# Queries, keys and probabilities of the forgetting heads turned in 32x32 blocks and carried through DRAM

## The reference, cut to what matters

```python
fq = rms_norm(fq.reshape(B, S, FOX_HEADS, 128), fox_q_g)   # queries, normed
fk = rms_norm(fk.reshape(B, S, FOX_HEADS, 128), fox_k_g)   # keys, normed
c = jnp.cumsum(log_sigmoid(flog + b_forget), axis=1)
s_f = einsum('bhqd,bhkd->bhqk', fq_b, fk_h) * fox_scale + cq_b[..., :, None] - ck[..., None, :]
p_f = softmax(where(causal, s_f, NEG_INF), axis=-1)
o_f = einsum('bhqk,bhkd->bhqd', p_f, fv_h)
```

## Time and profile before

| | us |
|---|---|
| median of 3 runs (1050.15 to 1050.65) | 1050.58 |
| the profiled execution | 1050.27 |
| its span, first to last instruction | 1048.5 |
| TensorE busy | 1044.0 |
| ScalarE busy | 778.0 |
| VectorE busy | 756.2 |

### The profile page before, as it was taken

The page is one execution under the profiler, slowest core; times in us unless marked ns, Lnnn a source line. Parts: engine busy times, 40 slices in busy tenths (PEclk is TensorE's granted clock), DMA queues, the critical chain, the costliest instruction groups (busy, mean ns, idle before and its releaser), DMA issues.

```text
span 1048.5 us, 16983 instructions
## 1 busy us (share of the span) xinstructions
PE 1044.0 (100%) x5495; PEld 950.2 (91%) x5495; DVE 756.2 (72%) x1259; ACT 778.0 (74%) x1334; POOL 35.8 (3%) x43
## 2 busy tenths in 40 slices
PE   9999999999999999999999999999999999999998
PEld 9999999999999988888888888888889988888887
DVE  7788877777668764586776776777767678777664
ACT  7777676888856544879788788797787778758853
POOL 0101020000002210000000000000000000000000
DMA  9755565565656666566665665665655766656664
GB/s 358 232 163 172 182 206 186 161 198 164 225 197 193 207 201 202 193 212 200 195 219 190 198 218 189 213 204 192 219 180 190 236 202 202 204 195 214 205 204 143
DMA packets 66939, 211.35 MB, mean 202 GB/s; under 512 B 9272, under 2 KB 10432, under 8 KB 66752
## 3 DMA queue, kind: packets, MB, share of 16 engines
q1 hardware_dynamic: 66880, 210.57, 62.0%
HBM read 208.43 MB, written 2.11 MB: 201 GB/s over the span
## 4 chain that ended last, share of the span: by engine, by line
PE 97%; ACT 1%; DVE 1%; issue 0%; DMA 0%; SPq 0%; DVEq 0%; ACTq 0%
PE ps L547 14%; PE ps L548 14%; PE ps L549 14%; PE ps L343 7%; PE ps L345 7%; PE ps L344 7%; PE ps L585 7%; PE ps L583 7%; PE ps L584 7%; PE ps L350 5%; PE ps L351 3%; PE ps L369 1%; PE ps L378 1%; ACT w_hi L631 1%; PE ps L454 0%; ACT qkT L677 0%
## 5 line engine op out<-in xcount | busy, mean ns | idle before, releaser
L1058 DVE TENSOR_TENSOR w_lo<-raw,w_hi 128x1024 fp32r<-128x1024 f32 (+1 forms) x406 | 463.4, 1148 | 228.0 <-ACT w_hi L631 225.5
L631 ACT ACTIVATE w_hi<-raw 128x1024 fp32r<-128x1024 f32 (+1 forms) x406 | 400.1, 988 | 182.5 <-PE ps L549 65.0
L547 PE MATMUL ps<-w_hi,xs 128*128 128x512 f32 (+1 forms) x704 | 263.5, 374 | 0.0
L548 PE MATMUL ps<-w_lo,xs 128*128 128x512 f32 (+1 forms) x704 | 263.4, 374 | 0.0
L549 PE MATMUL ps<-w_hi,xs 128*128 128x512 f32 (+1 forms) x704 | 263.4, 374 | 0.0
L343 PE MATMUL ps<-w_hi,xs 128*128 128x384 f32 (+1 forms) x512 | 172.6, 337 | 0.0
L344 PE MATMUL ps<-w_lo,xs 128*128 128x384 f32 (+1 forms) x512 | 167.0, 326 | 0.0
L345 PE MATMUL ps<-w_hi,xs 128*128 128x384 f32 (+1 forms) x512 | 167.0, 326 | 0.0
L549 PEld LDWEIGHTS ps<-w_hi,xs 128*128 128x128 f32 x704 | 133.1, 189 | 17.2
L548 PEld LDWEIGHTS ps<-w_lo,xs 128*128 128x128 f32 x704 | 133.1, 189 | 17.2
L547 PEld LDWEIGHTS ps<-w_hi,xs 128*128 128x128 f32 x704 | 133.1, 189 | 17.1
(11 more groups left out here) (158 smaller groups left out, 948.9 us busy)
## 6 DMA issues: line engine op xcount, KB each, us to landing
raw<-in_wrest SPq DMA_DIRECT2D x278, 512.0 KB, 4.1
raw<-in_win SPq DMA_DIRECT2D x117, 384.0 KB, 3.5
raw<-in_wrest SPq DMA_DIRECT2D x16, 384.0 KB, 3.0
xtok<-in_xtok SPq DMA_DIRECT2D x4, 512.0 KB, 13.5
raw_ahead<-in_w SPq DMA_DIRECT2D x5, 392.0 KB, 7.9
xv<-in_xT SPq DMA_DIRECT2D x7, 256.0 KB, 7.5
out<-x_tok SPq DMA_DIRECT2D x7, 256.0 KB, 4.3
raw_ahead<-in_win SPq DMA_DIRECT2D x3, 384.0 KB, 8.4
```

Of the source, the lines that this page charges most:

```text
L547: pe.matmul(o, xh, wh, start=(k == 0), stop=False, skip_group_check=True)
L548: pe.matmul(o, xh, wl, start=False, stop=False, skip_group_check=True)
L631: act.activation(slot(w_hi, s, w), slot(raw, s, w), ACT.Copy).then_inc(hi_ready, 1)
L1058: dve.tensor_tensor(slot(w_lo, s, w), slot(raw, s, w), f32(slot(w_hi, s, w)), ALU.subtract).then_inc(split_done, 1)
```

## The change

- Head 9 joins the scheme of blocks: it is turned by VectorE, no longer by TensorE, and its steps get the places of the other block heads. Scores move from after piece 5 to after piece 6.
- `norm_apply` writes the queries and keys with the four 32-column groups outermost, so that each group's blocks are contiguous after the turn. `turn_qk` moves behind the split of b = 7.
- The 16 copies of `move_qk` go. ScalarE instead issues one DMA of the turned tile to DRAM (`store_qk`, after the split of b = 1), waits for it, and issues four DMAs back, one per group of 32 partitions (`load_qkT`, b = 2). The keys are read by the scores as they land; the queries are copied once into a contiguous tile (`copy_q`, b = 4).
- The probabilities of heads 9 to 14 are no longer turned by TensorE: `normalise` writes them in block order, VectorE turns them (`turn_p`, at b = 7 between `norm_stats` and `norm_apply`), SP stores them to DRAM and loads them back in four DMAs (`store_p`, `load_pT`), in between its loads of weights, and the values are multiplied after piece 4 of the next frame instead of piece 1. Head 15's probabilities stay with TensorE.
- SP's loop over the weight pieces is written out from piece 76 on.

```diff
-BLOCK_AT = dict(scores=5)
-MOVES = {1: (0, 5), 2: (5, 10), 3: (10, 15)}
-FOX1_AT = dict(turn=2, scores=3, probs=6, values=7)
+BLOCK_AT = dict(scores=6)
+QK0, P_STOP = H + 1, HEADS - 1
...
+            def store_p(f):
+                sp.wait_ge(p_turned, blocks_counted(f))
+                if f > QK0:
+                    sp.wait_ge(pT_landed, 64 * blocks_counted(f - 1))
+                sp.dma_start(p_d, pdT[:]).then_inc(p_stored, 16)
+
+            def load_pT(f):
+                sp.wait_ge(p_stored, 16 * blocks_counted(f))
+                sp.wait_ge(pv_done, f - 1)
+                for j in range(4):
+                    src = p_d[:, j * 3 * 32:(j + 1) * 3 * 32].rearrange("(i r) c -> r i c", i=4)
+                    sp.dma_start(pT[32 * j:32 * (j + 1), :].rearrange("r (i c) -> r i c", i=4), src).then_inc(pT_landed, 16)
+
+            one_piece(8 * QK0 + 4)
+            one_piece(8 * QK0 + 5)
+            for f in range(QK0, HEADS):
+                one_piece(8 * f + 6)
+                if f > QK0:
+                    store_p(f - 1)
+                    load_pT(f - 1)
+                for g in range(8 * f + 7, 8 * f + 14):
+                    one_piece(g)
...
+            def block_scores(f):
+
+                pe.wait_ge(qkT_ready, f)
+                k = qkT[:].rearrange("p (i n m t) -> p n m i t", i=4, m=M, n=2)[:, 1]
+                for qb in range(M):
+                    last = pe.matmul(bank(B_S, qb * P, (qb + 1) * P), qT[:, qb * P:(qb + 1) * P], k[:, 0:qb + 1], start=True,
+                                     stop=True, skip_group_check=True)
+                last.then_inc(s_done, 1)
+
+            def block_values(f, p):
+
+                pe.wait_ge(pT_landed, f * 64 - 64 * (QK0 - 1))
+                pe.wait_ge(mixlo_done, f - 1)
...
-                    if spill and b == 0:
-                        prob_transposes(f - 1, "fox")
-                    if spill and b == 1:
-                        values(f - 1, par, "fox")
+                    if spill and b == 4:
+                        block_values(f - 1, par)
...
+            def store_qk(f):
+                act.wait_ge(qk_turned, f - (QK0 - 1))
+                if not (isinstance(f, int) and f == QK0):
+                    act.wait_ge(qk_landed, f * 64 - 64 * QK0)
+                act.dma_start(qk_d, qnT[:]).then_inc(qk_stored, 16)
+
+            def load_qkT(f):
+                act.wait_ge(qk_stored, f * 16 - 16 * (QK0 - 1))
+                act.wait_ge(s_done, f - 1)
+                for j in range(4):
+                    src = qk_d[:, j * 4 * 32:(j + 1) * 4 * 32].rearrange("(i r) c -> r i c", i=4)
+                    act.dma_start(qkT[32 * j:32 * (j + 1), :].rearrange("r (i c) -> r i c", i=4), src).then_inc(qk_landed, 16)
+
+            def copy_q(f):
+
+                act.wait_ge(qk_landed, f * 64 - 64 * (QK0 - 1))
+                turned = qkT[:].rearrange("p (i n m t) -> p n m i t", i=4, m=M, n=2)
+                act.activation(qT[:].rearrange("p (m i t) -> p m i t", m=M, i=4), turned[:, 0], ACT.Copy).then_inc(qkT_ready, 1)
...
                     if b == 7:
                         evacuate(f * 8 + 8, par, par)
-                        if next_kind == "diff" or blocks:
-                            head_norm(f + 1, next_kind)
...
+                        head_norm(f + 1, next_kind)
                     split_next(f, b, PW if last and b >= 4 else W1)
...
+                    if at is BLOCK_AT and b == 1:
+                        store_qk(f)
+                    if at is BLOCK_AT and b == 2:
+                        load_qkT(f)
+                    if at is BLOCK_AT and b == 4:
+                        copy_q(f)
+                    attention_steps(f, kind, b, at)
                     if trail:
                         trailing_steps(f, b)
...
+            def turn_p(f):
+
+                dve.wait_ge(p_ready, f)
+                if not (isinstance(f, int) and f == QK0):
+                    dve.wait_ge(p_stored, f * 16 - 16 * QK0)
+                dve.transpose(pdT[:], pd[:]).then_inc(p_turned, 1)
...
                 for b in range(8):
-                    before_split(f, kind, b, at, trail)
+                    before_split(f, kind, b, at, trail, p_blocks)
                     if b == 7:
                         norm_stats(f + 1, next_kind)
-                        norm_apply(f + 1, 1 - p, next_kind)
-                        if turn:
-                            turn_qk(f + 1, 1 - p)
+                        if p_blocks:
+                            turn_p(f)
+                        norm_apply(f + 1, 1 - p, next_kind, blocks=turn)
...
                     split_next(f, b, PW if last and b >= 4 else W1)
+                    if turn and b == 7:
+                        turn_qk(f + 1, 1 - p)
```

More of the change, by code:

```diff
@@ L301, in _, with one_piece @@
                          ).then_inc(cq_landed, 16)
-            with sp.Fori(17, IN_PIECES // RING) as i:
+            with sp.Fori(17, 2 * QK0 + 1) as i:
                 in_pieces(i)
+            def one_piece(g):
+                sp.wait_ge(split_done, g - RING + 1)
+                if g < IN_PIECES:
+                    sp.dma_start(slot(raw, g % RING, W1), win_d[(g - 8) * P:(g - 7) * P, :]).then_inc(raw_landed[g % RING], 16)
+                else:
+                    sp.dma_start(slot(raw, g % RING), wrest_d[(g - IN_PIECES) * P:(g - IN_PIECES + 1) * P, :]
+                                 ).then_inc(raw_landed[g % RING], 16)
+            def store_p(f):
[18 more added lines that the diff above has]
+                    one_piece(g)
+            one_piece(OUT0 + 6)
+            one_piece(OUT0 + 7)
             sp.dma_start(conv[:], vec_d).then_inc(conv_landed, 16)
@@ L371, in scores @@
                 last.then_inc(s_done, 1)
+            def block_scores(f):
[8 more added lines that the diff above has]
+                pe.wait_ge(mixlo_done, f - 1)
+                v = [qkv[:, (p * M + m) * QKV + 2 * HD:(p * M + m + 1) * QKV] for m in range(M)]
+                turned = pT[:].rearrange("p (i s t) -> p s i t", i=4, s=3)
+                pe.matmul(bank(B_O, 0, S), v[0], turned[:, 0:2], start=True, stop=False, skip_group_check=True)
+                pe.matmul(bank(B_O, P, P), v[1], turned[:, 2], start=False, stop=True,
+                          skip_group_check=True).then_inc(pv_done, 1)
             def prob_transposes(f, kind):
@@ L417, in attention_steps @@
                 if b == at["scores"]:
-                    scores(f, kind)
+                    if at is BLOCK_AT:
+                        block_scores(f)
+                    else:
+                        scores(f, kind)
                 if b == at.get("probs"):
@@ L498, in _ @@
                 frame(f, f % 2, "diff", DIFF_AT, trail=True, late=f == 4, forget=f == 5)
-            frame(H + 1, 1, "fox", FOX1_AT, trail=True)
-            frame(H + 2, 0, "fox", BLOCK_AT)
+            frame(H + 1, 1, "fox", BLOCK_AT, trail=True)
+            frame(H + 2, 0, "fox", BLOCK_AT, spill=True)
             with pe.Fori(H // 2 + 1, H - 1) as i:
@@ L662, in copy_qkT @@
             def copy_qkT(f, kind):
-                act.wait_ge(tp_done, H + 2 if isinstance(f, int) and f == HEADS else f)
+                act.wait_ge(tp_done, H + 1 if isinstance(f, int) and f == HEADS else f)
                 if kind == "fox":
@@ L759, in split_next, with frame @@
                 split_hi(f * 8 + (b + 4), b % RING, f * 2 + (2 + b // 4), w)
-            def frame(f, par, kind, next_kind, at=None, trail=False, last=False, forget=False, blocks=False, spill=False):
+            def frame(f, par, kind, next_kind, at=None, trail=False, last=False, forget=False, spill=False):
                 for b in range(8):
@@ L1121, in norm_apply @@
                         src = qkv[:, (p * M + m) * QKV + j * w:(p * M + m) * QKV + (j + 1) * w]
+                        gain = row[:, R_FG + j * w:R_FG + (j + 1) * w]
                         i = m * 2 + j
-                        last = dve.scalar_tensor_tensor(
-                            out=qn[:, (p * 2 * M + i) * w:(p * 2 * M + i + 1) * w], in0=src, scalar=rs[:, i:i + 1],
-                            in1=row[:, R_FG + j * w:R_FG + (j + 1) * w], op0=ALU.mult, op1=ALU.mult)
+                        to = qn[:, (p * 2 * M + i) * w:(p * 2 * M + i + 1) * w]
+                        if blocks:
+                            src, gain = [a.rearrange("p (j t) -> p j t", j=4) for a in (src, gain)]
+                            to = qn[:, p * 2 * M * w:(p + 1) * 2 * M * w].rearrange("p (j n t) -> p n j t", j=4, n=2 * M)[:, j * M + m]
+                        last = dve.scalar_tensor_tensor(out=to, in0=src, scalar=rs[:, i:i + 1], in1=gain, op0=ALU.mult,
+                                                        op1=ALU.mult)
                 last.then_inc(normed, 1)
@@ L1158, in normalise @@
                         lo, w = qb * P, P * (1 + qb)
-                        last = dve.tensor_scalar(s_sb[:, lo:lo + w], s_sb[:, lo:lo + w], rl[:, qb:qb + 1], None, ALU.mult)
```

(5 more changed lines are left out.)

73 lines of the change are left out of this document (31 added, 42 removed).

## The result

The changed kernel takes 1074.4 us (median of 6 runs) against 1050.62, a ratio of 1.0226 with a 95% interval of 1.0212 to 1.0240. The forecast was 1049.3. One of the six took 1368.4 us at a mean granted clock of 0.753, where the others had 0.990 to 0.995; it is left out of the ratio, and the other five alone have a median of 1073.8. The span of the profiled execution is 1073.1 us, 24.6 more than before.

The account below looks back on a forecast made before the run. TensorE, busy 1044.0 of 1048.5 us, was taken as the bound. 1050.27 - 2.42 (transposes) - 0.3 (late copies) + 1.45 (wait at head 8's end) = 1049.0, plus 0.3 for the runs' median: 1049.3 us, range 1047.6 to 1054.

Parts of the forecast that it names:

- What TensorE sheds: TensorE's stream: 22 transposes go, 2.42 us, and a wait of 0.3; scores and values in block order cost nothing extra.
- rival D: TensorE: each transpose is worth its whole record, 0.27 us, 22 of them 6.0, giving 1045.7 us; chance 0.02.
- What VectorE gets: VectorE at a frame's end: turn of probabilities 0.53 us added; the split of b = 7 keeps a lead of 0.65.
- Rival C: VectorE's lead at b = 7 is gone; TensorE waits 0.1 to 0.65 us per frame, 1049.9 to 1053.2; chance 0.17.
- The probabilities' way: SP's store and four loads back: store 2.2 us, landing 2.5, in time for the values with a lead of 1.3.
- Head 8's end: Frame 9: ScalarE's guess comes behind store and loads, so TensorE waits 1.45 us before transposing head 8's result.
- The queries' way: ScalarE's store and four loads back of queries and keys: copied near E+12.5, needed at E+14.3, lead 1.8 us.
- E: Time origin of the forecast's deadlines: the end of a frame's last piece on TensorE, just before ScalarE's squares start.
- head 10's late copies: TensorE's wait for ScalarE's 16 late copies at the first head, 0.3 us, claimed to go with the copies.
- covered by 3 us: SP's next weight load, delayed by the probabilities' transfers, lands at E+9.5 to 10 and is still in time by 3 us.
- Rival B: Slow read-back from DRAM: probabilities land late, TensorE waits 2.15 us at the values in six frames, 1062 us; chance 0.12.

Follow-up runs that it names:

- e2: Changed kernel with only the probabilities of heads 9 to 14 through DRAM; queries and keys by TensorE and ScalarE's 16 copies as before: 1050.5 us, ratio 1.0001.
- e6: e2 with head 15 in its old places (queries and keys turned before the split, scores after piece 5): 1050.35 us, ratio 1.0000.
- e3: Changed kernel with weight pieces 76 to 127 loaded only in their first 96 of 768 columns: 1052.6 us, single execution.
- e12b: Changed kernel with weight pieces 76 to 127 loaded only in 384 of 768 columns: 1053.25 us, single execution.
- e1: Changed kernel with only queries and keys through DRAM; probabilities of 9 to 15 turned by TensorE as before: 1062.7 us, ratio 1.0112.
- e5: Changed kernel with the queries' store and read-back moved to SP's queue, among its weight loads: 1065.4 us, ratio 1.0136.
- e7: Changed kernel with 6 matmuls into an unused bank in front of each TensorE wait for the queries: 1072.3 us, ratio 1.0199.

## Why the prediction was wrong

**What TensorE sheds: right.** 0.33 us per frame, measured in e2. A transpose is worth 0.11 us of path, not its record (rival D falls). Scores and values cost the same in block order (0.67 and 0.66 us; e2).

**What VectorE gets: right.** The lead at b = 3 was narrow and held, though the turn of the probabilities took 0.58 us, not 0.53: 0.2 us was lost once in e2, and 0.73 where both turns stood ahead of the split (e6). Rival C is real but was not in the changed kernel's list of waits.

**The probabilities' way: right, and better.** Store 1.9 us (2.2 forecast), read-back 1.9 (2.5).

**Head 8's end: right in place and cause, short in size.** 2.1 us in place of 1.45. Four issues took 1.78 us (1.65), but they began at 177.34, not 175.95: the store of the first head took 3.4 us to land, not 2.2, again beside three weight loads (2.1 in e3, with thin ones). That would have made nearly 3 us of wait. That it was only 2.1 is in part luck: head 8's values, six matmuls that take 0.66 us of TensorE at the start of frame 9, are missing from the forecast's "after five pieces at 168.1 + 9.75", and TensorE came that much later too.

**The queries' way: the step that failed.** ScalarE "issues four loads until E+9.7, which have landed near E+12", with a lead of 1.8. All but the landing came true: in the frame shown above (E = 208.5) the loads left from E+8.2 to E+10.1, but the last landed at E+17.1. The term of 2.5 us for a landing was an estimate from transfers that ran alone. It measured 5.6 us by the median and up to 7.4, and the waits were 14.2 us in six heads; the 0.3 us credited for head 10's late copies turned into one of them. Two things were left out. The loads share the engines with the weights, and e3, e12b and the changed kernel show the landing rising from 2.2 over 3.5 to 5.6 us as the weights do. And the probabilities' detour, which the forecast checked only for its own deadline and the weights' ("covered by 3 us"), holds the weights back until they leave together, just ahead of these loads; e1 puts that at 1.2 us of landing and about half of the waits. The forecast counted DMA time in the weights' direction only, never what weights do to a small transfer. The DMA engines' share of 0.65 in these frames, not much over 0.59, gave no warning: a mean over a frame says nothing of the three microseconds in which one transfer has to pass.

The Trainium skill's "DMA: Bandwidth & Descriptors" (Issuing engines are not separate DMA queues) says that DMAs started by different engines run on the same 16 DMA engines and interleave. The trace agrees (5.6 us beside the weights, 2.2 without), and weighed in the forecast it would have asked for just this term.

**Rival B: the right kind, the wrong transfer.** It gave 1062 for a slow way back, with 0.12, and put it on the probabilities. Its threshold of 3.8 us is that of the probabilities (2.5 and their lead of 1.3), and they stayed below it; the same sum for the queries gives 2.5 + 1.8 = 4.3, which the changed kernel passes. The rows it used, 5.9 and 6.2 us, had been dismissed in part because one read was queued behind the other. That company may be what they had in common with the queries' loads; no run tests it.

**The clock: not foreseen.** No term of the forecast had it. Once TensorE waits, the granted clock falls in some frames (0.92, 0.85) and not in others (1.00 at 231.90, in spite of a wait): it fell after the waits of 1.9, 3.2, 2.9 and 2.4 us and not after those of 1.5 and 2.2. That adds about 10 us to 16.3 of waits. The executions of e1 show such a price by themselves: the two with a clock of 1.000 took 1060.9 and 1061.2 us, the two with 0.996 and 0.998 took 1064.3 and 1064.5.

## What to carry to other kernels

A small transfer with a deadline must be priced by what is in flight on every queue when it leaves, not by the landing of one that ran alone and not by the mean share of the DMA engines. When a change adds a round trip on a queue that also prefetches, look for what the prefetch does afterwards: it comes in a burst and lands on whoever is next. And try the halves of a change apart; here one gave 1.1 us and the other cost 12 alone and more together.

## What the runs showed of the hardware

- The same kind of DMA, 48 or 64 KB in 128 rows into 32 partitions, landed in 1.9 us where no more than one weight load was in flight when it left (the probabilities, and e5) and in 5.6 us with three or four 384 KB loads out on another queue. Fewer and longer rows changed 0.4 us of that.
- A DMA issue took 0.31 to 0.62 us of ScalarE's queue, median 0.45, for four-by-32 rows, and 0.55 us of GpSimd's. ScalarE's arithmetic behind it waited: the guess of head 8 started at 179.17, after four issues of 1.78 us in all, and at 176.52 where it stood ahead of them.
- In four of six frames with waits of 1.5 to 3.2 us the granted clock went to its lower level (1.2 in place of 2.4 GHz), 20.5 us in all, which costs about 10 us beside 16.3 of waits. With the waits filled in part (e7) it was 6.8 us. What decides between one frame and another was not settled.
